# Hybrid decoder layer on one core: product 5 divided once more in group 18, with the reload of its quarter of x moved inside the group

## The chip, the cores and the metric

The kernel runs on one core of one Trainium2 chip. The metric is the device time of one execution in microseconds (us). Before the change the median of three runs is 1356.91 us, the lowest 1356.5 and the highest 1358.13.

## What is computed

One layer on x of 1024 tokens by 1024 features, all in float32:

```python
h = rmsnorm(x, norm_g[layer])
proj = h @ w_in[layer]                      # 1024 x 12288
b_a, c_a, x_a, z_a, q, k, v, z_b, g_a, g_b = split(proj)
y_a = short_conv_branch(b_a, c_a, x_a, z_a, conv_w, conv_b, w_a_out)
y_b = retention_branch(q, k, v, z_b, w_b_out)
x = x + (sigmoid(g_a) * y_a + sigmoid(g_b) * y_b) @ w_o
return rmsnorm(x, final_g)
```

The change touches only how a few columns of `h @ w_in` are computed.

## The kernel before, in words

**Products.** Every large matrix product is done by a Strassen-Winograd scheme: the matrix is cut in quadrants and seven products stand in for eight. Each float32 operand is split in a high and a low part, and a product is the sum of three matmuls (high by high, high by low, low by high; lines 2746, 2748 and 2749). The high part of the weights is made by ScalarE (`high`, line 1211), the low part by VectorE (`low`, lines 1755 and 1758), into three rotating slots: the parts of unit u can be made only when TensorE is done with unit u-3.

**Groups.** After the columns of v, the other columns of `w_in` are done in 20 groups (0 to 19) of 512 columns. Groups 0 and 1 hold a gate ("gate" groups), 2 to 9 the convolution ("conv"), 10 to 17 q, k and z_b ("turn": rotary turning and silu), 18 and 19 the other gate. In each group TensorE does the products in the order 1, 6, 2, 5, 7, 3, 4. A plain product is one unit of 24 matmuls of 512 columns.

**Divided products.** Some products are themselves cut in quarters and done by seven products of quarters: 42 matmuls of 256 columns, in two halves of 18 and 24, each with its own unit of weights (lines 2664 to 2666). Product 4 is divided in groups 1 to 18 (`TWICE`), product 3 in 2 to 9 (`THIRDS`), product 5 in 2 to 17 (`FIFTHS`). For a divided product POOL makes four sums of quarters of the weights (`second_sums`, lines 1027 to 1032) before the second half's parts can be made, and VectorE subtracts the shared quarters from the results (`second_first`, line 1913, once; `second_rest`, line 1926, three instructions) before it adds the product itself (`add`, lines 1905 and 1907).

**The x side.** Dividing product 5 needs four combinations of quarters of its x operand, T1 to T4. T3 takes the place of the operand's own quarter 1 in SBUF; the own quarter is kept in DRAM (`kept_d[2]`) and must be back before a plain product 5 runs. T1, T2 and T4 of products 4 and 5 share one area, `hx`: in each group of `FIFTHS` the ones of product 5 are loaded (`load_hx(5)`, lines 717 and 718, 0.5 and 1 MB) once product 4 of the group before has ended, and the ones of product 4 (`load_hx(4)`) once product 5 of this group has ended. TensorE waits for them by `t4_in` and `t1_t2_in`.

**Order of the work.** All orders are written out by hand. SyncE issues most transfers from one queue: in group g the parts of the next group's weights (line 628) as their buffers come free, and the stores of the results of group g-1 (`turn_stores`, lines 649, 700 and 701; `gate_stores`, line 649). ScalarE and VectorE each run one list in which unit u's place also carries work of the group before. Where `g in FIFTHS`, that list is another one: VectorE puts the turning of group g-1 in other places, and does `add(g, 3)` only behind `second_first` of product 4; ScalarE does the high parts of group g-1's second turn one unit later. ScalarE's evacuation of product 2 (`c11`, lines 1348 and 1349 in a turn group, line 1353 with a sigmoid in a gate group) stands at the unit of product 5; the high parts of the unit after next are made ahead of it, and those of the next unit again behind it. TensorE's product 7 waits for `c11_read`, product 3 for `add(g, 5)`, product 4 for `add(g, 7)`.

**After the groups.** From inside group 19 on the retention runs step by step. Its first transfers of q and k (`load_step`, line 784) wait until all stores of q, k and of group 18's gates have landed; its first scores (line 2782) are computed between products 5 and 7 of group 19.

Of the kernel before, what the change touches and what calls it, by code (L numbers as in the profile page):

```python
# [6 lines left out]
F32 = mybir.dt.float32  # L7
# [38 lines left out]
GROUPS = 20  # L46
# [2 lines left out]

TWICE = range(1, GROUPS - 1)  # L50
THIRDS = CONVS
FIFTHS = range(2, GROUPS - 2)
LAST_HALF, THIRD_HALF, FIFTH_HALF = 7, 8, 9
UNIT_TABLE = [(g, p) for g in range(GROUPS) for p in (0, 1, 2, 3, FIFTH_HALF, 4, 5, 6, LAST_HALF, THIRD_HALF)
              if (p != THIRD_HALF or g in THIRDS) and (p != LAST_HALF or g in TWICE) and (p != FIFTH_HALF or g in FIFTHS)]
UNITS = VALUE_UNITS + len(UNIT_TABLE)
# [49 lines left out]
def unit_at(g, product):  # L106
    return VALUE_UNITS + UNIT_TABLE.index((g, ORDER.index(product)))


def ended_at(g):  # L110

    return unit_at(g, 4) + (g in TWICE)


def third_ended_at(g):

    return VALUE_UNITS + UNIT_TABLE.index((g, THIRD_HALF if g in THIRDS else 5))


def fifth_ended_at(g):  # L120

    return unit_at(g, 5) + (g in FIFTHS)

# [6 lines left out]
def halved_product(g, product):  # L130

    return product == 4 and g in TWICE or product == 3 and g in THIRDS or product == 5 and g in FIFTHS

# [25 lines left out]
def summed_until(g):  # L159

    return 16 + g + (g > 0) + 4 * len([n for n in TWICE if n < g]) + 4 * len([n for n in THIRDS if n < g])\
        + 4 * len([n for n in FIFTHS if n < g])


def s2_made(g):

    return summed_until(g) + 1 + (g == 0)


def second_summed(g, product, n):  # L170

    return summed_until(g) + 1 + 4 * (product != 5 and g in FIFTHS) + 4 * (product == 3) + n


def second_added(g, product, n):

    before_g = 20 + 4 * (g - TWICE.start) + 4 * len([f for f in THIRDS if f < g])\
        + 4 * len([f for f in FIFTHS if f < g or f == g and product != 5])
    if g not in THIRDS or product == 5:
# [27 lines left out]
def kind_of(g):  # L207
    return "conv" if g in CONVS else "turn" if g in QZS else "gate"
# [123 lines left out]
def build(nc, x_t, columns, w_value, w_channel, w_last, x_rows, final_g, rope, tables, identity, out):  # L332
# [8 lines left out]
    kept_d = nc.dram_tensor("kept_scratch", (4, P, 2, 2, QUARTER), F32, kind="Internal").ap()  # L341
# [7 lines left out]
    def sem(name):  # L349
        return held.enter_context(nc.semaphore(name))  # L350
# [87 lines left out]
    w_hi, w_ready, unit_done = sem("w_hi"), sem("w_ready"), sem("unit_done")  # L438
# [45 lines left out]
    fifth_kept, t4_in, t1_t2_in = x_start, x_in[5], x_in[6]  # L484
# [26 lines left out]
    def made(name, count=2):  # L511

        return (8 if name == "raw" else 12) + 2 * MADE.index(name) + count

    def x_quarter(product, n, part):

        return hc[:, KEPT_AT[product], part, 2 * (n // 2):2 * (n // 2) + 2, n % 2 * QUARTER:(n % 2 + 1) * QUARTER]
# [40 lines left out]
    def _(sp):  # L558
# [67 lines left out]
        def load_work(g, role, quadrant):  # L626
            n = ROLES[g][role]
            sp.dma_start(work[n][:, :], w_channel[g, quadrant]).then_inc(work_in[n], 16)
# [86 lines left out]
        def load_hx(product):  # L715
            n = int(product == 5)
            sp.dma_start(hx[:, 2].bitcast(F32), hx_d[n, :, 2]).then_inc(t4_in, 16)
            sp.dma_start(hx[:, 0:2].bitcast(F32), hx_d[n, :, 0:2]).then_inc(t1_t2_in, 16)

        for g in range(GROUPS):  # L720
            if g == 1:
                sp.wait_ge(h_ready, made(3) + 4)
                for part, a in enumerate((t5_high, t5_low)):
                    sp.dma_start(hx_d[1, :, :, part], a[:, 0:3]).then_inc(fifth_kept, 16)
                    sp.dma_start(kept_d[3, :, part], a[:, 3]).then_inc(fifth_kept, 16)
                sp.wait_ge(fifth_kept, 112)
                sp.wait_ge(h_ready, made(3) + 4 + 3)
                sp.dma_start(hx_d[0], hx[:, :].bitcast(F32)).then_inc(fifth_kept, 16)
            if g == FIFTHS.start:
                sp.wait_ge(unit_done, unit_at(g - 1, 5) + 1)  # L730
                sp.wait_ge(fifth_kept, 128)
                for part in range(2):
                    sp.dma_start(x_quarter(5, 1, part).bitcast(F32), kept_d[3, :, part]).then_inc(fifth_kept, 16)
            if g in FIFTHS:
                sp.wait_ge(unit_done, ended_at(g - 1) + 1)
                load_hx(5)
            if g == FIFTHS.stop:
                sp.wait_ge(unit_done, fifth_ended_at(g - 1) + 1)
                for part in range(2):
                    sp.dma_start(x_quarter(5, 1, part).bitcast(F32), kept_d[2, :, part]).then_inc(fifth_kept, 16)  # L740
            if g == THIRDS.start:
                stores[kind_of(g - 1)](g - 1)
            if g + 1 < GROUPS:
                sp.wait_ge(w_ready, unit_at(g, 2) + 1)
                sp.wait_ge(summed, s2_made(g))
                load_work(g + 1, "a", 0)
            if g == TWICE.stop:
                sp.wait_ge(unit_done, ended_at(g - 1) + 1)
                for part in range(2):
                    sp.dma_start(x_quarter(4, 1, part).bitcast(F32), kept_d[0, :, part]).then_inc(kept_in, 16)  # L750
            if g == THIRDS.stop:
                sp.wait_ge(unit_done, third_ended_at(g - 1) + 1)
                for part in range(2):
                    sp.dma_start(x_quarter(3, 1, part).bitcast(F32), kept_d[1, :, part]).then_inc(third_kept, 16)
            if g + 1 < GROUPS:
                sp.wait_ge(w_ready, fifth_ended_at(g) + 1)
                load_work(g + 1, "e", 3)
                if g in FIFTHS and g in THIRDS:
                    sp.wait_ge(unit_done, fifth_ended_at(g) + 1)
                    load_hx(4)  # L760
                sp.wait_ge(w_ready, unit_at(g, 7) + 1)
                load_work(g + 1, "b", 2)
                if g in THIRDS and g > THIRDS.start:
                    stores[kind_of(g - 1)](g - 1)
                if g in FIFTHS and g not in THIRDS:
                    sp.wait_ge(unit_done, fifth_ended_at(g) + 1)
                    load_hx(4)
                if g in THIRDS:
                    sp.wait_ge(w_ready, ended_at(g) + 1)
                    load_work(g + 1, "d", 3)  # L770
                sp.wait_ge(w_ready, third_ended_at(g) + 1)
                load_work(g + 1, "c", 1)
            if g and g not in THIRDS:
                stores[kind_of(g - 1)](g - 1)
            if g + 1 < GROUPS and g not in THIRDS:
                sp.wait_ge(w_ready, ended_at(g) + 1)
                load_work(g + 1, "d", 3)
            if g == QZS.start:
                sp.wait_ge(y_out, 16 * len(CONVS))
                sp.dma_start(rope_sb[:, :, :], rope).then_inc(rope_in, 16)  # L780
# [2237 lines left out]
```

## Time and profile before

| | |
|---|---|
| median of 3 runs | 1356.91 us |
| profiled execution, its own time | 1357.59 us |
| its span | 1355.8 us |
| TensorE busy | 1344.9 us (99%) |
| VectorE, ScalarE, POOL busy | 1102.3, 622.7, 381.6 us |
| moved by DMA | 310.35 MB, mean 229 GB/s |

Times in rows are us from the start of the span, durations us as well unless ns is written. Matmul ends are modelled and overlap the next one, so the pace of TensorE is read from starts: from one matmul's start to the next one's. "ACT" is ScalarE, "DVE" VectorE, "SPq" SyncE's sequencer when it issues a DMA. In brackets stands how long the engine was idle before the instruction, and what released it.

### The profile page before, as it was taken

What the parts mean: (1) busy time and instruction counts of PE and PEld (TensorE: products, weight loads), DVE (VectorE), ACT (ScalarE), POOL (GpSimd) and SP (SyncE); (2) the same over time, 40 slices, a digit from 0 to 9 for tenths busy, and PEclk for the clock granted to TensorE, in tenths of its full rate; (3) what the DMA queues carried; (4) which work ended last, traced back from release to release, by engine and by line L of the source; (5) the groups of instructions that cost most, each with busy time, mean ns of one, the idle gap of its engine ahead of it and who ended that gap; (6) DMA issues with size and microseconds to landing.
All of it is one profiled execution on the core that took longest, in us unless ns stands there. A gap on an engine that the chain in (4) does not pass through costs nothing.

```text
span 1355.8 us, 18174 instructions
## 1 busy us (share of the span) xinstructions
PE 1344.9 (99%) x6930; PEld 1150.5 (85%) x6930; DVE 1102.3 (81%) x1179; ACT 622.7 (46%) x844; POOL 381.6 (28%) x411
## 2 busy tenths in 40 slices
PE   9999999999999999999999999999999999999997
PEld 8788888888898899888888888888888888888886
DVE  6898575688888888789999898748776998788887
ACT  7843243433333343333434443448778433434445
POOL 0100112344444554233343342225444001100002
PEclk9999999999999999999999999999999999999999
DMA  9746477867777777789999999866767689945443
GB/s 336 216 133 213 139 218 223 264 204 207 198 217 229 218 232 233 254 234 267 281 282 267 290 286 292 256 218 248 270 218 260 157 325 306 235 154 202 163 86 125
DMA packets 130534, 310.35 MB, mean 229 GB/s; under 512 B 9488, under 2 KB 54160, under 8 KB 121360
## 3 DMA queue, kind: packets, MB, share of 16 engines
q1 hardware_dynamic: 118928, 260.41, 55.0%
q0 software_dynamic: 11376, 48.76, 19.7%
q8 instruction: 55, 0.90, 0.3%
q14 instruction: 31, 0.25, 0.1%
q10 hardware_dynamic: 144, 0.02, 0.0%
HBM read 241.00 MB, written 59.77 MB: 222 GB/s over the span
## 4 chain that ended last, share of the span: by engine, by line
PE 88%; DVE 3%; ACT 2%; SPq 2%; issue 2%; DMA 2%; POOL 1%; POOLq 0%; DVEq 0%; ACTq 0%
PE psum L2748 12%; PE psum L2746 12%; PE psum L2749 12%; PE psum L2891 7%; PE psum L2889 7%; PE psum L2890 7%; PE psum L2664 5%; PE psum L2666 5%; PE psum L2665 5%; PE psum L2653 3%; PE psum L2655 3%; PE psum L2656 3%; PE psum L2791 2%; PE psum L2793 2%; PE psum L2792 2%
## 5 line engine op out<-in xcount | busy, mean ns | idle before, releaser
L1211 ACT ACTIVATE slots<-work 128x1024 fp32r<-128x1024 f32 (+1 forms) x182 | 182.4, 1011 | 407.4 <-POOL work L1032 145.8
L2748 PE MATMUL psum<-hc,slots 128*128 128x512 f32 x784 | 305.2, 389 | 0.0
L2746 PE MATMUL psum<-hc,slots 128*128 128x512 f32 x784 | 305.2, 389 | 0.0
L2749 PE MATMUL psum<-hc,slots 128*128 128x512 f32 x784 | 305.1, 389 | 0.0
L1504 ACT ACTIVATE last_slot<-arena 128x1024 fp32r<-128x1024 f32 x112 | 118.8, 1063 | 163.0 <-PE psum L2891 157.2
L2889 PE MATMUL psum<-last_slot 128*128 128x512 f32 (+1 forms) x452 | 175.3, 388 | 0.0
L2891 PE MATMUL psum<-last_slot 128*128 128x512 f32 (+1 forms) x452 | 175.0, 387 | 0.0
L2890 PE MATMUL psum<-last_slot 128*128 128x512 f32 (+1 forms) x452 | 175.0, 387 | 0.0
L2749 PEld LDWEIGHTS psum<-hc,slots 128*128 128x128 f32 x784 | 147.2, 188 | 30.8
L2746 PEld LDWEIGHTS psum<-hc,slots 128*128 128x128 f32 x784 | 147.2, 188 | 29.4
L2748 PEld LDWEIGHTS psum<-hc,slots 128*128 128x128 f32 x784 | 147.2, 188 | 29.3
L2094 DVE TENSOR_TENSOR last_slot<-arena,last_slot 128x1024 fp32r<-128x1024 f32 x112 | 135.8, 1223 | 31.1 <-ACT last_slot L1504 30.5
L1758 DVE TENSOR_TENSOR slots<-work,slots 128x1024 fp32r<-128x1024 f32 x116 | 136.6, 1183 | 13.4 <-ACT slots L1211 13.1
L2890 PEld LDWEIGHTS psum<-last_slot 128*128 128x128 f32 x452 | 84.9, 188 | 17.4
L2889 PEld LDWEIGHTS psum<-last_slot 128*128 128x128 f32 x452 | 84.9, 188 | 17.4
L2891 PEld LDWEIGHTS psum<-last_slot 128*128 128x128 f32 x452 | 84.9, 188 | 17.2
L2666 PE MATMUL psum<-hc,slots 128*128 128x256 f32 x336 | 94.9, 282 | 0.0
L2665 PE MATMUL psum<-hc,slots 128*128 128x256 f32 x336 | 94.7, 282 | 0.0
L2664 PE MATMUL psum<-hc,slots 128*128 128x256 f32 x336 | 94.6, 282 | 0.0
L2653 PE MATMUL psum<-slots,hc 128*128 128x512 f32 x224 | 88.3, 394 | 0.5 <-DVE slots L1758 0.5
L1755 DVE SCALAR_TENSOR_TENSOR slots<-work,slots 128x1024 fp32r<-128x1024 f32 (+1 forms) x66 | 75.6, 1146 | 16.1 <-ACT slots L1211 16.1
L1027 POOL TENSOR_TENSOR work<-work 128x256 f32<-128x256 f32 x42 | 39.8, 948 | 169.0 <-DVE slots L1755 109.8
(230 smaller groups left out, 2755.5 us busy)
## 6 DMA issues: line engine op xcount, KB each, us to landing
work<-w_channel SPq DMA_DIRECT2D x99, 512.0 KB, 5.4
hx<-hx_scratch SPq DMA_DIRECT2D x32, 1024.0 KB, 8.8
work<-w_channel POOLq DMA_DIRECT2D x59, 512.0 KB, 6.9
arena<-w_last SPq DMA_DIRECT2D x19, 1024.0 KB, 7.6
hx<-hx_scratch SPq DMA_DIRECT2D x32, 512.0 KB, 6.1
qk<-qk_scratch SPq DMA_DIRECT2D x32, 512.0 KB, 3.7
arena<-w_last POOLq DMA_DIRECT2D x9, 1024.0 KB, 11.3
v_raw<-value_scratch SPq DMA_DIRECT2D x32, 256.0 KB, 4.0
```

The source lines that it names most:

```text
L1211: nc.scalar.activation(slots[:, u % SLOTS, 0, 0:columns_of(u)], src, ACT.Copy, scale=-1.0 if negated(u) else 1.0).then_inc(w_hi, 1)
L1758: nc.vector.tensor_tensor(slot[:, 1, :], src, slot[:, 0, :].bitcast(F32), ALU.subtract).then_inc(w_ready, 1)
L2094: nc.vector.tensor_tensor(slot[:, 1, :, :], pair_at(group, product, j), slot[:, 0, :, :].bitcast(F32), ALU.subtract).then_inc(last_ready, 1)
L2664: nc.tensor.matmul(to, slot[:, 0, w], high, start=start and j == 0, stop=False, skip_group_check=True)
L2665: nc.tensor.matmul(to, slot[:, 0, w], low, start=False, stop=False, skip_group_check=True)
L2666: last = nc.tensor.matmul(to, slot[:, 1, w], high, start=False, stop=j == 1, skip_group_check=True)
L2746: nc.tensor.matmul(bank, slot[:, 0, w], x_high, start=product in STARTS and j == 0, stop=False, skip_group_check=True)
L2748: nc.tensor.matmul(bank, slot[:, 0, w], x_low, start=False, stop=False, skip_group_check=True)
L2749: last = nc.tensor.matmul(bank, slot[:, 1, w], x_high, start=False, stop=j == 3, skip_group_check=True)
L2889: nc.tensor.matmul(bank, l_high, r_high, start=start, stop=False, skip_group_check=True)
L2890: nc.tensor.matmul(bank, l_high, r_low, start=False, stop=False, skip_group_check=True)
L2891: return nc.tensor.matmul(bank, l_low, r_high, start=False, stop=stop, skip_group_check=True)
```

## The change

`FIFTHS` gains group 18, so that every place in the kernel that asks `g in FIFTHS` or `halved_product(g, 5)` now answers yes there. The load that brings product 5's own quarter back was issued first thing in group `FIFTHS.stop` (18); it is now issued in the last group of `FIFTHS` (again 18), behind `load_hx(4)`, and serves the plain product 5 of group 19.

```diff
@@ -49,7 +49,7 @@
 
 TWICE = range(1, GROUPS - 1)
 THIRDS = CONVS
-FIFTHS = range(2, GROUPS - 2)
+FIFTHS = range(2, GROUPS - 1)
 LAST_HALF, THIRD_HALF, FIFTH_HALF = 7, 8, 9
@@ -734,10 +734,6 @@
             if g in FIFTHS:
                 sp.wait_ge(unit_done, ended_at(g - 1) + 1)
                 load_hx(5)
-            if g == FIFTHS.stop:
-                sp.wait_ge(unit_done, fifth_ended_at(g - 1) + 1)
-                for part in range(2):
-                    sp.dma_start(x_quarter(5, 1, part).bitcast(F32), kept_d[2, :, part]).then_inc(fifth_kept, 16)
             if g == THIRDS.start:
                 stores[kind_of(g - 1)](g - 1)
@@ -765,6 +761,9 @@
                 if g in FIFTHS and g not in THIRDS:
                     sp.wait_ge(unit_done, fifth_ended_at(g) + 1)
                     load_hx(4)
+                if g == FIFTHS.stop - 1:
+                    for part in range(2):
+                        sp.dma_start(x_quarter(5, 1, part).bitcast(F32), kept_d[2, :, part]).then_inc(fifth_kept, 16)
                 if g in THIRDS:
                     sp.wait_ge(w_ready, ended_at(g) + 1)
                     load_work(g + 1, "d", 3)
```

## Rows read from the trace of the kernel before

**Rows 1.** The page: busy time by engine, and TensorE's granted clock in 40 slices.

```profile
PE 1344.9 (99%) x6930; PEld 1150.5 (85%) x6930; DVE 1102.3 (81%) x1179; ACT 622.7 (46%) x844; POOL 381.6 (28%) x411
...
PEclk9999999999999999999999999999999999999999
```

**Rows 2.** Windows of units, groups 17 and 18: length, busy by engine, clock, DMA, GB/s.

```profile
807.96:812.89 4.93, 4.93 (x44) 4.93 (x42) 4.49 (x7) 4.02 (x6) 0.15 (x1) 1.00 0.42 113
812.89:823.78 10.89, 10.89 (x50) 9.01 (x49) 10.58 (x13) 1.91 (x2) 5.76 (x6) 1.00 0.94 295
823.78:828.72 4.94, 4.94 (x44) 4.93 (x43) 4.27 (x6) 2.63 (x4) 0.29 (x1) 1.00 1.09 331
...
845.06:850.50 5.44, 5.44 (x26) 4.50 (x25) 4.61 (x7) 4.41 (x5) 0.00 (x0) 1.00 0.38 72
```

**Rows 3.** Timeline of ScalarE, group 17: start, length, instruction, idle before.

```profile
809.64 0.62 ACT L1388 ACTIVATE turn_b<-turn_a 128x512 fp32r<-128x512 f32 x1
...
811.12 1.05 ACT L1211 ACTIVATE slots<-work 128x1024 fp32r<-128x1024 f32 x1
...
824.88 0.62 ACT L1388 ACTIVATE turn_b<-turn_a 128x512 fp32r<-128x512 f32 x1
825.41 1.04 ACT L1211 ACTIVATE slots<-work 128x1024 fp32r<-128x1024 f32 x1
```

**Rows 4.** Timeline of ScalarE, group 18.

```profile
846.74 0.61 ACT L1388 ACTIVATE turn_b<-turn_a 128x512 fp32r<-128x512 f32 x1
847.37 1.28 ACT L1353 ACT_TABLE_LOAD   x1
848.67 1.03 ACT L1353 ACTIVATE tp_c<-psum 128x1024 f32<-128x1024 f32 x1
...
859.34 1.06 ACT L1361 ACTIVATE tp_v<-tp_v 128x1024 f32<-128x1024 f32 x1 [0.56 <-DVE tp_v L1907]
```

**Rows 5.** Timeline of VectorE, group 17 and the first unit of group 18.

```profile
812.21 1.23 DVE L1755 SCALAR_TENSOR_TENSOR slots<-work,slots 128x1024 fp32r<-128x1024 f32 x1 [0.36 <-ACT slots L1211]
813.35 2.46 DVE L1926 TENSOR_TENSOR tp_first<-tp_first,psum 128x768 f32<-128x768 f32 x3
815.92 1.23 DVE L1905 TENSOR_TENSOR tp_v<-psum,tp_first 128x1024 f32<-128x1024 f32 x1
...
820.82 1.21 DVE L1907 TENSOR_TENSOR tp_v<-tp_v,psum 128x1024 f32<-128x1024 f32 x1
...
824.23 1.22 DVE L1755 SCALAR_TENSOR_TENSOR slots<-work,slots 128x1024 fp32r<-128x1024 f32 x1
...
827.05 1.22 DVE L1758 TENSOR_TENSOR slots<-work,slots 128x1024 fp32r<-128x1024 f32 x1
...
832.33 1.23 DVE L1758 TENSOR_TENSOR slots<-work,slots 128x1024 fp32r<-128x1024 f32 x1
```

**Rows 6.** Timeline of POOL, groups 17 and 18.

```profile
818.10 1.10 POOL L1027 TENSOR_TENSOR work<-work 128x256 f32<-128x256 f32 x1 [4.47 <-DVE slots L1755]
...
821.58 0.74 POOL L1032 TENSOR_TENSOR work<-work 128x256 f32<-128x256 f32 x1
...
828.43 2.71 POOL L1014 TENSOR_TENSOR work<-work,work 128x1024 f32<-128x1024 f32 x1 [5.19 <-DVE slots L1758]
```

**Rows 7.** Timeline of SyncE's queue, groups 17 and 18; last, all 32 loads of line 718.

```profile
813.46 0.43 SPq L718 DMA_DIRECT2D hx<-hx_scratch  x1
...
833.59 1.07 SPq L740 DMA_DIRECT2D hc<-kept_scratch  x2
...
DMA to landing us min/median/max: 6.1/8.8/11.6
```

**Rows 8.** Timelines of SyncE's queue and of TensorE, group 19.

```profile
872.29 0.36 SPq L649 DMA_DIRECT2D gate_scratch<-tp_v  x1
879.32 0.33 SPq L784 DMA_DIRECT2D qk<-qk_scratch  x1
...
888.08 0.28 PE L2782 MATMUL psum<-qk 128*128 128x256 f32 x1
```

## The prediction

> **What bounds the kernel now.** I read the page first: TensorE is busy 99% of the span, at the full clock (the upper level, 2.4 GHz) in all 40 slices [rows 1]. So time goes only if TensorE gets less to do, and comes only if something makes it wait. The windows of the units come next [rows 2]. A divided unit takes 4.93 us (product 5 of group 17), a plain one 5.44 us (product 5 of group 18); two plain ones take 10.89, and busy equals length in every window: no bubble anywhere. Beside it the reader should see VectorE: in the two units behind product 5 of group 17 it is busy 10.58 of 10.89 us. That stretch decides what the change gives, so the timelines of ScalarE, VectorE and POOL come last [rows 3 to 6].
>
> Group 17 is turned into a ruler. Its product 5 starts at 807.96, that of group 18 at 845.05 to 845.06, so group 17's clock plus 37.10 is group 18's. I give the times of group 18 after the change on group 17's clock: group 18 will do what 17 does (both also finish a turn group), except where its own kind, gate, differs.
>
> **The saving.** One plain product (5.44) becomes one divided (4.93): -0.51 us of TensorE. The row of group 17 prices it, with the operands, queue and engines it will have in group 18.
>
> **What is added and hidden.** POOL makes four more sums, about 4.2 us by the same four behind product 4 (818.10 to 821.58 + 0.74) [rows 6], in the idle time that group 17 uses for them. ScalarE and VectorE make one more pair of parts; VectorE subtracts quarters four times more. All that is in group 17's timeline, which shows no wait of TensorE, so it costs nothing by itself. What hides it is VectorE's last slack.
>
> **The transfers.** SyncE issued the two reload DMAs at 833.59, 1.07 us together [rows 7]. In that place now stand the two of `load_hx(5)`, so the queue there is as long as before; landing at most 11.6 us after about 834.1 gives 845.7, and T1 is wanted at 845.06 + 2.11 = 847.2 (18 of the 42 matmuls, 18/42 x 4.93 = 2.11). `load_hx(4)` is issued at 813.46 + 37.10 = 850.56 for its 1 MB part, and wanted by the second half of product 4 at 845.06 + 4.93 + 10.89 + 2.11 = 862.99: 12.4 us, against 8.8 in the median and 11.6 at worst of 32 loads [rows 7]. The reload goes past the loads of parts a, e and b to stand behind it; it lands some 20 us before group 19's product 5. Queued behind its 1.07 us are part c of group 19, wanted some 20 us later, and the stores of group 17. Those slip by several us, and with them the wait before the first q and k load. That wait ended last on group 18's last gate store, issued at 872.29, the load following at 879.32, and the scores that need it come at 888.08 [rows 8]. The store will come about 2.5 us later (below); the load then goes out near 881.8 and takes some 4 to 7 us, before 889. Cost zero, 0 to 1 in the bounds.
>
> **Where group 18 differs from 17: the sigmoid.** ScalarE evacuates product 2 at the unit of product 5. In group 17 these are two short instructions between 809.64 + 0.62 and 811.12 [rows 3]. In group 18 a table load of 1.28 us comes first, then one of 1.03: from 847.37 to 849.70 [rows 4], or 812.60 on group 17's clock. Product 7 waits for it and is now due at 812.89: 0.3 us to spare, no cost. But ScalarE's next work, the high part for product 3, starts at 812.50 instead of 811.12: 1.38 later. Today that is free, since nobody on VectorE needs it early; in the divided order VectorE makes the low part of product 3 *ahead of* `second_rest` of product 5. In group 17 it was already waiting for ScalarE (0.36 us, low part at 812.21) and then ran without a gap to the low part of product 4's second half [rows 5]. So 1.39 us of delay travel down the whole run:
>
> 1. `second_rest` 813.35 becomes 814.74; `add(5)` 815.92 to 817.15 becomes 817.31 to 818.54. Product 3 wants it at 812.89 + 5.44 = 818.33. With some 0.05 for the handover TensorE waits **0.25 us**.
> 2. `add(7)` ends at 822.03 + 1.39 = 823.42; product 4 wants it at 823.78 + 0.25: no wait.
> 3. The low part of product 4's second half, 824.23 to 825.45, becomes 825.62 to 826.84. Wanted at 824.03 + 2.11 = 826.14: a wait of **0.75 us**.
> 4. The low part of product 1 of group 19 (827.05 to 828.27 in the ruler) needs ScalarE's high part, 825.41 in the ruler. It is later by 1.39, and by one gate instruction of 1.06 that a gate group puts ahead of it [rows 3, 4]: 827.80 to 828.85. Low part 828.88 to 830.10; wanted at 828.72 + 1.00 = 829.72. A wait of **0.42 us**.
> 5. The low part of product 6 needs POOL's S2, which runs 2.71 us behind step 4's low part [rows 6]: 830.25 to 832.96; high part to 834.0, low part to 835.4 (832.33 + 1.23 = 833.56 in the ruler [rows 5]). Wanted at 830.14 + 5.44 = 835.58: 0.2 us to spare. From there VectorE has no turning left and catches up.
>
> The sum: -0.51 + 0.25 + 0.75 + 0.42 = **+0.91 us**. The bounds of the waits: 0 if the 1.39 is absorbed (total -0.51), and for a longer chain the second-worst is every spare of 0.2 to 0.3 gone too (+0.7, total +1.6). I take the middle, since each term follows from rows of the same instructions. Against the profiled execution: 1357.59 + 0.91 = 1358.50. That execution lay 0.68 above the median, so as a median 1356.91 + 0.91 = **1357.8 us**. About 0.2% (2.7 us) is what a measurement of this kernel can tell from no change; the forecast lies within.
>
> **Rivals.**
>
> *A, the saving arrives whole.* If ScalarE's lateness does not reach TensorE, the time is 1356.91 - 0.51 = 1356.4. For it: group 17 has no wait at all, and a shift of VectorE against its neighbours may change how long its instructions take. Against it: VectorE had 0.31 us idle in those 10.89. Chance 0.22, with cases in between.
>
> *B, the table switch costs more than its row.* In the row the sigmoid starts 0.02 us behind the end of the table load (847.37 + 1.28, then 848.67) [rows 4]. If a further pause as long as the load came with it where the engine is pressed, all of steps 1 to 3 would start 1.28 us later: product 7 would wait 1.0 (812.60 + 1.28 against 812.89), product 3 then 0.5, the second half of product 4 0.7, and product 1 of group 19 0.4 as before. 1.0 + 0.5 + 0.7 + 0.4 - 0.5 = +2.1, so 1359.0. The Trainium skill, "ScalarE: Activation LUTs", section "What ACT_TABLE_LOAD costs", states such a pause: 1283 ns for the load plus about 1380 ns of drain, 2.66 us in all. The trace agrees on the load and shows no drain between it and the sigmoid. Chance 0.04.
>
> *C, slower: the exchange of combinations lands late.* The 1 MB of T1 and T2 for product 4 shares the engines with what is issued behind it: reload 0.5 MB, part c 0.5, four silu stores 1.0, q and k stores another 1.0 and more. At the 295 GB/s of that window [rows 2] 2 MB take 6.8 us, 3 MB 10.2. Served alongside, the load lands at 850.56 + 8.8 + 6.8 = 866.2 or at 869.6, TensorE waits 3.2 to 6.6 us, and the time is 1359.6 to 1363.0. It decides once the landing takes over 15.6 us; against it stands that 32 of 32 took at most 11.6 with the same company, bar the 0.5 MB. Chance 0.05.
>
> **How the numbers follow.** Forecast 0.62; A 0.22; B 0.04; C 0.05; small mixtures with an extra wait in group 19 but within 0.2% 0.05; a gain over 0.2% through some realignment that I don't see 0.02. Same: 0.62 + 0.22 + 0.04 + 0.05 = 0.93. Slower 0.05, faster 0.02. The range holds A with the scatter of the runs (0.4 below the median): 1356.4 - 0.5 = 1355.9, and B with as much scatter and a little of another wait: 1359.0 + 0.6 = 1359.6.
>
> **What the changed profile would show.** Product 5 of group 18 in 42 matmuls over 4.93 us; no table load but the one at about 847.4; `second_rest` of product 5 at 851.8 instead of 850.5; windows of group 18 with gaps of TensorE of about 0.25 ahead of product 3 (near 855.4), 0.75 inside product 4 (near 863.2) and 0.4 ahead of group 19's product 1 (near 866.8); group 19's product 1 starting 0.9 later than 866.30; all of it kept to the end. Line 718's new loads within 12 us. I am wrong if group 19 begins before 866.3, if a wait ends on a DMA, or if a gap opens in group 19 or at the first scores.

## The result, and the profile after

The changed kernel takes **1359.79 us** in the median of 12 runs (1358.55 to 1362.34); the kernel before, timed beside it, 1356.95. The ratio is 1.0023, with a 95% interval of 1.0015 to 1.003: about 0.2% slower, 2.8 us. The forecast was 1357.8 within 1355.9 to 1359.6, so the median lies 0.2 us above the range.

The windows of the changed kernel (columns as in [rows 2]): first group 18 and the part of group 19 up to the first scores, then product 5, products 7 and 3, and product 4 of group 18.

```profile
828.27:866.73 38.46, 37.84 (x206) 32.37 (x204) 33.52 (x39) 16.07 (x19) 13.64 (x12) 1.00 0.92 288
866.73:890.46 23.73, 22.06 (x96) 17.97 (x97) 13.86 (x14) 10.28 (x11) 3.60 (x2) 1.00 0.89 264
...
844.61:849.54 4.93, 4.93 (x43) 4.93 (x42) 2.97 (x5) 4.70 (x6) 0.89 (x1) 1.00 0.38 111
849.54:860.87 11.33, 11.18 (x50) 8.94 (x49) 10.40 (x11) 1.83 (x3) 4.68 (x5) 1.00 0.95 317
860.87:866.73 5.86, 5.38 (x43) 4.98 (x41) 4.75 (x8) 3.67 (x5) 0.30 (x1) 1.00 1.10 340
```

The same two stretches of the kernel before:

```profile
828.72:866.30 37.58, 37.58 (x188) 31.95 (x187) 30.47 (x35) 16.77 (x19) 11.29 (x9) 1.00 0.89 247
866.30:888.08 21.78, 21.78 (x99) 18.02 (x97) 10.54 (x10) 8.17 (x9) 1.07 (x2) 1.00 0.95 310
```

Product 5 is down to 4.93 us, as group 17's row said. But products 7 and 3 take 11.33 instead of 10.89 (+0.44), product 4 takes 5.86 instead of 4.93 (+0.93), and from the start of group 19 to the first scores 23.73 us pass instead of 21.78 (+1.95). The sum is -0.51 + 0.44 + 0.93 + 1.95 = +2.8 us, as much as the medians differ. These are the rows of one execution, of 1360.26 us. (The spans, 1358.3 against 1355.8, differ by 2.5: this execution came to group 18 0.45 us earlier and lost 0.1 us behind the first scores.) Group 18 alone costs 0.9 us net; group 19, which the diff hardly touches, costs twice that.

TensorE in the timeline shows where the waits end:

```profile
855.30 0.47 PE L2745 MATMUL psum<-hc,slots 128*128 128x512 f32 x1
...
863.53 0.38 PE L2663 MATMUL psum<-hx,slots 128*128 128x256 f32 x1 [0.36 <-DVE slots L1754]
...
866.73 0.50 PE L2745 MATMUL psum<-hc,slots 128*128 128x512 f32 x1
...
890.46 0.36 PE L2781 MATMUL psum<-qk 128*128 128x256 f32 x1 [1.67 <-DMA qk<-qk_scratch]
```

Lines stand one lower than before. Product 3 started 0.14 us behind the end of `add(5)` (853.93 + 1.23 in the rows below), the second half of product 4 waited for VectorE's low part, group 19's product 1 for the next low part, and the first scores for the transfer of q and k.

Each wait costs a little more than its gap. Behind it the first two matmuls start 0.31 to 0.34 us apart where 0.23 is usual (512 columns), or 0.22 where 0.12 is usual (256 columns). Read from starts, the gaps themselves are 0.30, 0.52, 0.27 and 1.83 us; about 0.1 us behind each makes up the rest.

ScalarE and VectorE in group 18 (timelines; they answer to [rows 3 to 5]):

```profile
846.93 1.28 ACT L1352 ACT_TABLE_LOAD   x1
848.22 1.03 ACT L1352 ACTIVATE tp_c<-psum 128x1024 f32<-128x1024 f32 x1
849.14 1.78 ACT L1210 ACTIVATE slots<-work 128x1024 fp32r<-128x1024 f32 x2
...
863.43 1.04 ACT L1360 ACTIVATE tp_v<-tp_v 128x1024 f32<-128x1024 f32 x1
864.38 1.04 ACT L1210 ACTIVATE slots<-work 128x1024 fp32r<-128x1024 f32 x1
```

```profile
850.23 1.22 DVE L1754 SCALAR_TENSOR_TENSOR slots<-work,slots 128x1024 fp32r<-128x1024 f32 x1 [1.73 <-ACT slots L1210]
851.37 2.46 DVE L1925 TENSOR_TENSOR tp_first<-tp_first,psum 128x768 f32<-128x768 f32 x3
853.93 1.23 DVE L1904 TENSOR_TENSOR tp_v<-psum,tp_first 128x1024 f32<-128x1024 f32 x1
...
862.26 1.22 DVE L1754 SCALAR_TENSOR_TENSOR slots<-work,slots 128x1024 fp32r<-128x1024 f32 x1
...
865.45 1.23 DVE L1757 TENSOR_TENSOR slots<-work,slots 128x1024 fp32r<-128x1024 f32 x1 [1.04 <-ACT slots L1210]
```

On group 17's clock the low part of product 3 starts at 850.23 - 37.10 = 813.13 in an execution that is 0.45 early, so 813.58: the forecast had 813.60. The sequence that VectorE then runs is the forecast's, to 0.1 us.

SyncE's queue, from the exchange (`load_hx(4)`) to the first step's load:

```profile
850.10 0.89 SPq L718 DMA_DIRECT2D hx<-hx_scratch  x1
...
867.31 0.85 SPq L649 DMA_DIRECT2D qk_scratch<-tp_v  x1
...
869.68 0.69 SPq L701 DMA_DIRECT2D qk_scratch<-turn_a  x1
870.42 1.14 SPq L628 DMA_DIRECT2D work<-w_channel  x1
871.60 0.97 SPq L746 DMA_DIRECT2D hc<-kept_scratch  x2
...
874.40 1.27 SPq L649 DMA_DIRECT2D gate_scratch<-tp_v  x1
887.00 0.33 SPq L783 DMA_DIRECT2D qk<-qk_scratch  x1
```

Group 18's last gate store goes out at 874.40, 2.1 us later than in [rows 8]; with the 0.45 that is the 2.5 of the forecast. But the load behind it goes out at 887.00, not 881.8: the store took 12.6 us to land instead of 7.0. In the kernel before, the second set of group 17's turn stores began at 858.21:

```profile
858.21 0.36 SPq L649 DMA_DIRECT2D qk_scratch<-tp_v  x1
```

Here it begins at 867.31, right ahead of part d, the reload of product 4's quarter and the gate stores. The windows of the transfers (last two columns: busy share of the 16 DMA engines, GB/s) show where the work went. The changed kernel:

```profile
855.00:860.00 5.00, 4.85 (x22) 3.90 (x22) 5.00 (x7) 0.00 (x0) 3.81 (x4) 1.00 1.03 406
...
875.00:880.00 5.00, 5.00 (x23) 4.13 (x22) 3.28 (x3) 2.11 (x3) 0.00 (x0) 1.00 0.99 265
```

The kernel before:

```profile
855.00:860.00 5.00, 5.00 (x23) 4.13 (x22) 4.30 (x5) 2.88 (x4) 4.29 (x5) 1.00 0.60 147
...
875.00:880.00 5.00, 5.00 (x24) 4.14 (x23) 2.36 (x2) 1.06 (x1) 0.00 (x0) 1.00 0.74 196
```

Before, the engines had idle time at 855 to 860 and again at 875 to 880, where SyncE sat waiting for a store that was nearly alone. After the change both stretches are full.

### The profile page after: what moved, and what is told of

The parts are those of the page before. It is cut to its first block, busy times and chain, and to the rows that moved or that the text cites. A ratio compares the mean times of both kernels' runs of the same rounds, so it can differ in the third digit from the quotient of the medians.

```text
span 1358.3 us, 18229 instructions
## 1 busy us (share of the span) xinstructions
PE 1345.3 (99%) x6948; PEld 1151.4 (85%) x6948; DVE 1107.6 (82%) x1184; ACT 621.7 (46%) x845; POOL 385.8 (28%) x415
## 4 chain that ended last, share of the span: by engine, by line
PE 91%; DVE 3%; DMA 2%; issue 2%; ACT 2%; POOL 1%; POOLq 0%; SPq 0%; DVEq 0%; ACTq 0%
PE psum L2747 12%; PE psum L2745 12%; PE psum L2748 12%; PE psum L2889 7%; PE psum L2890 7%; PE psum L2888 7%; PE psum L2663 5%; PE psum L2665 5%; PE psum L2664 5%; PE psum L2652 4%; PE psum L2655 4%; PE psum L2654 4%; PE psum L2790 2%; PE psum L2792 2%; PE psum L2791 2%
## 5 line engine op out<-in xcount | busy, mean ns | idle before, releaser
L2745 PE MATMUL psum<-hc,slots 128*128 128x512 f32 x776 | 302.3, 390 | 0.3
L2747 PE MATMUL psum<-hc,slots 128*128 128x512 f32 x776 | 302.1, 389 | 0.0
L2748 PE MATMUL psum<-hc,slots 128*128 128x512 f32 x776 | 302.0, 389 | 0.0
L2748 PEld LDWEIGHTS psum<-hc,slots 128*128 128x128 f32 x776 | 145.7, 188 | 30.5
L2745 PEld LDWEIGHTS psum<-hc,slots 128*128 128x128 f32 x776 | 145.7, 188 | 29.9 <-issue 0.5
L2747 PEld LDWEIGHTS psum<-hc,slots 128*128 128x128 f32 x776 | 145.7, 188 | 28.9
L2665 PE MATMUL psum<-hc,slots 128*128 128x256 f32 x344 | 97.2, 282 | 0.0
L2664 PE MATMUL psum<-hc,slots 128*128 128x256 f32 x344 | 96.9, 282 | 0.0
L2663 PE MATMUL psum<-hc,slots 128*128 128x256 f32 x344 | 96.9, 282 | 0.0
L2652 PE MATMUL psum<-slots,hc 128*128 128x512 f32 x224 | 88.2, 394 | 0.0
L2655 PE MATMUL psum<-slots,hc 128*128 128x512 f32 x224 | 87.2, 389 | 0.0
```

The lines of the kernel that those rows point to most:

```text
L2652: nc.tensor.matmul(bank, x_high, w_high, start=product in starts and i == 0 and kk == 0, stop=False, skip_group_check=True)
L2655: last = nc.tensor.matmul(bank, x_low, w_high, start=False, stop=i == 1 and kk == 1, skip_group_check=True)
L2663: nc.tensor.matmul(to, slot[:, 0, w], high, start=start and j == 0, stop=False, skip_group_check=True)
L2664: nc.tensor.matmul(to, slot[:, 0, w], low, start=False, stop=False, skip_group_check=True)
L2665: last = nc.tensor.matmul(to, slot[:, 1, w], high, start=False, stop=j == 1, skip_group_check=True)
L2745: nc.tensor.matmul(bank, slot[:, 0, w], x_high, start=product in STARTS and j == 0, stop=False, skip_group_check=True)
```

## The experiments

Each was timed in five rounds beside the kernel before on the same chip; that kernel's median there stands beside it. "Wait at the scores" is the length from group 19's first matmul to the first scores, less the 21.78 us of the kernel before.

Two questions were put apart, the waits in group 18 and the wait at the scores. **D**: the table load ahead of the sigmoid makes VectorE late, which gives the three waits in group 18. It is the forecast's own. For the wait at the scores three theories stood: W (3 MB more bytes), Q (SyncE's wait for the gate stores), O (group 17's turn is finished later in the divided order, so its stores fall on the others).

### e1_table_early: no table load on the critical stretch

```diff
                         silu(g - 1, 3)
+                        if g == QZS.stop:
+                            nc.scalar.activation(small[:, 41:42], eps[:, 0:1], ACT.Sigmoid)
```

> The changed kernel, but ScalarE does a sigmoid of one column behind the second silu of group 17's results (early in group 18), so that the table load of 1.28 us falls in an idle stretch there and no longer ahead of the sigmoid of product 2. Theory D (the divided order puts VectorE's low part of product 3, and with it second_rest and all behind it, behind the table load): the waits of TensorE ahead of product 3 (0.44 us) and inside product 4 (0.55) vanish, the one ahead of group 19's product 1 (0.38) shrinks to 0 to 0.1, so group 18 takes 37.1 us instead of 38.46; the wait at the first scores of group 19 (1.7 to 1.9) stays or grows, since the gate stores have less time: 1 us or so is gained, about 1358.8 as a median. Rival (the waits come from the transfers or from POOL's four more sums): group 18 stays at 38.4 us and the time at 1359.8.

Measured: 1361.44 us (6 runs) against 1357.18, ratio 1.0031 (1.0019 to 1.0043). Its windows and its table load:

```profile
828.66:865.76 37.10, 37.10 (x207) 32.40 (x205) 33.66 (x39) 16.27 (x20) 13.63 (x12) 1.00 0.93 285
865.76:890.11 24.35, 21.98 (x98) 17.91 (x97) 14.49 (x14) 10.27 (x11) 3.60 (x2) 1.00 0.93 280
```

```profile
836.61 1.28 ACT L1644 ACT_TABLE_LOAD   x1
```

Group 18 takes 37.10 us without a gap: all three waits are gone at once, by moving 1.28 us of ScalarE. D is shown. And nothing came of it: the first scores start at 890.11 instead of 890.46, with 2.57 us of wait instead of 1.95, because the q and k load comes when it comes. The 1 us of gain that I expected was missed. The median is even higher than the changed kernel's, though the two intervals overlap. The profiled execution, at 1359.8 us, is the fastest of the six. The other five took 1361.2 to 1361.6 us, and their mean granted clock is 0.997 where its own is 0.998. A stretch at TensorE's lower clock behind the longer wait, as it is seen in e14_small_deferred below, could do that, but no trace shows it here.

### e2_qk_early: the first load no longer waits for the gate stores

```diff
-        sp.wait_ge(tp_out[0], 16 * tp_stored(GROUPS - 2))
+        sp.wait_ge(tp_out[0], 16 * tp_stored(GROUPS - 4))
...
             load_step(s)
+        sp.wait_ge(tp_out[0], 16 * tp_stored(GROUPS - 2))
         stores[kind_of(GROUPS - 1)](GROUPS - 1)
```

> The changed kernel, but the first four loads of q, k and v wait for the stores of group 16 and 17 only (and for all stores of q and k), not for group 18's gate stores; the wait for those stands behind the four loads. Theory Q (the 1.95 us lost in group 19 are the first load of q and k, held back by the landing of group 18's last gate store): the load goes out near 880 instead of 887.0, lands before 888.8, TensorE has no wait at the first scores, and the time is 1.9 us less, about 1357.8 (the forecast's number). Rival (the load would be late anyway, since the queues are full of group 17's stores): load issued before 883 but landed after 889, gain under 0.5 us.

Measured: 1358.18 against 1357.18, ratio 1.0009 (1.0 to 1.0018). The load went out at 878.22 and took 9.4 us (3.9 in the kernel before); the wait at the scores is 21.90 - 21.78 = 0.1 us. Q holds: some 1.8 of the 2.8 us are back. What is left of the median is about group 18's net cost. (In this profile group 18 took 39.5 us, with a wait ahead of product 7 that e11_turn_early explains below.)

### e3_both and e4_before_both

> Both edits together on the changed kernel. Theories D and Q together: no wait in group 18 (37.1 us) nor at the first scores; the saving of 0.51 us arrives whole, 1356.4 us as a median, ratio to the kernel before 0.9996. Rival: some third cause, then at least 0.5 us of wait stays in groups 18 or 19.

> Control: both edits on the kernel before, product 5 of group 18 plain. Both theories: nothing, since that kernel has neither wait: group 18 takes 37.6 us, 1356.9 us, ratio 1.000. If it is faster by 1 us or more, the edits bring something of their own and e3_both says nothing of the change.

Measured: e3_both 1357.77, ratio 1.0002 (0.9994 to 1.0011); e4_before_both 1357.16 against the same 1357.18, ratio 1.0001 (0.9993 to 1.001). So the edits bring nothing by themselves, and on the changed kernel they take back nearly all. The window of e3_both from group 19 to the scores:

```profile
866.47:889.15 22.68, 21.99 (x98) 17.90 (x97) 12.81 (x13) 9.87 (x11) 3.60 (x2) 1.00 1.01 309
```

Group 18 is at 37.10, but 0.9 us go at the scores: the load went out at 877.90 and landed 11.1 us later, in queues that are busy all the time (share 1.01). The 0.51 us did not arrive; 1356.4 was missed.

### e5_no_exchange and e6_no_reload: fewer bytes

Both leave out transfers, so one product runs on the wrong combination or quarter of x and the layer's result is not computed; only their times are used.

```diff
                     sp.wait_ge(unit_done, fifth_ended_at(g) + 1)
-                    load_hx(4)
+                    if g != FIFTHS.stop - 1:
+                        load_hx(4)
```

(with `hx_loads(18, 4)` one lower), and for e6_no_reload:

```diff
-                if g == FIFTHS.stop - 1:
-                    for part in range(2):
-                        sp.dma_start(x_quarter(5, 1, part).bitcast(F32), kept_d[2, :, part]).then_inc(fifth_kept, 16)
...
-                pe.wait_ge(fifth_kept, 192)
+                pe.wait_ge(fifth_kept, 160)
```

> The changed kernel with load_hx(4) of group 18 left out (1.5 MB): product 4 of group 18 is computed with product 5's T1, T2 and T4, all its work and its waits stay. Theory W (the q and k load is late because 3 MB more go through queues that are full from 850 us on, so that everything behind them lands later): the last gate store lands several us earlier, the first q and k load goes out before 884 instead of 887, the wait at the first scores falls from 1.7 to 0.3 at most, the time by 1.3 to 1.9 us to 1358.0 to 1358.5. Rival O (the stores of group 17 are late because the divided order turns its second half later on VectorE and ScalarE, whatever the bytes): the load goes out at 886 or later, the wait stays over 1 us, the time over 1359.2. Group 18 itself keeps its 38.4 us by both.

> The changed kernel with the reload of product 5's own quarter left out (0.5 MB, two transfers of SyncE): the plain product 5 of group 19 runs on T3 in its place. Theory W: a third of the effect of leaving out the 1.5 MB, a gain of 0.3 to 0.7 us. Rival (the place of the reload, behind the exchange and ahead of group 17's stores, is what costs): the gain is 1.5 us or more. Theory O: no gain.

Measured: 1359.61 and 1359.9 against 1357.45, ratios 1.0012 (1.0003 to 1.002) and 1.0013 (1.0002 to 1.0024). Queue and window of e5_no_exchange:

```profile
875.66 1.21 SPq L649 DMA_DIRECT2D gate_scratch<-tp_v  x1
887.62 0.33 SPq L784 DMA_DIRECT2D qk<-qk_scratch  x1
```

```profile
868.18:891.07 22.89, 22.05 (x96) 17.97 (x97) 13.02 (x13) 10.03 (x11) 3.61 (x2) 1.00 0.82 244
```

With 1.5 MB less the last gate store still takes 12 us to land, the load still goes out at 887.6, and 1.1 us of wait remain (0.9 in e6_no_reload, with its load at 888.27). Group 18 keeps its 38.5 us in both. The medians are 2.2 and 2.5 us above the kernel before. W is not the main cause; whether the bytes have a part of 0.3 to 1 us can't be told, since the ratios' intervals overlap the changed kernel's, and 0.5 MB left out does as much as 1.5.

### e9_before_late_turn: one part of the change alone

On the kernel before, ScalarE's and VectorE's splitting of group 17's second turn is put where the divided order has it, and nothing else:

```diff
-                    if p == (5 if g in FIFTHS else 4):
+                    if p == (5 if g in FIFTHS or g == QZS.stop else 4):
                         turned(g - 1, 1)
...
                     second_first(g, product_at(n))
+                    if n == 6 and g == QZS.stop:
+                        turned(g - 1, 1)
...
-                    if p == 4 and g not in FIFTHS:
-                        turned(last, 1)
```

> The kernel before, product 5 of group 18 plain, with one part of the change alone: in group 18 the second half of group 17's turn is split in parts as late as the divided order does it (ScalarE one unit later, VectorE behind second_first of product 4), so that its four stores of q and k (1 MB in packets of 512 bytes) go out at 866 to 869 instead of 858 to 861, right ahead of part d, the reload and group 18's gate stores. Theory O: the last gate store, issued at 872 to 874, lands 10 us or more later; the first q and k load goes out at 883 or later instead of 879.3; TensorE waits 0.3 to 1.5 us at the first scores, the time rises by as much, to 1357.3 to 1358.5. Rival W (bytes): nothing changes, load at 879 to 880, no wait.

Measured: 1360.42 against 1357.83, ratio 1.0019 (1.0002 to 1.0035): 2.6 us slower. The profiled execution is the slowest of the twelve (1367.98 us; the others took 1358.46 to 1366.53). It lost 6.5 us at about 697 to 706, long before group 18 and the edit: a wait of 3.0 us for VectorE, then TensorE at half its clock (0.50) until about 706. So its times in group 18 stand 6.5 us later. Windows, queue, and the row of TensorE's waits:

```profile
835.26:872.85 37.59, 37.59 (x189) 31.96 (x188) 30.41 (x34) 16.52 (x19) 10.97 (x9) 1.00 0.86 230
872.85:896.83 23.98, 21.94 (x99) 17.87 (x97) 13.78 (x14) 9.22 (x10) 1.06 (x2) 1.00 0.78 232
```

```profile
874.20 0.36 SPq L649 DMA_DIRECT2D qk_scratch<-tp_v  x1
...
880.82 0.73 SPq L649 DMA_DIRECT2D gate_scratch<-tp_v  x1
893.17 0.33 SPq L784 DMA_DIRECT2D qk<-qk_scratch  x1
```

```profile
PE psum L2782 <- DMA qk<-qk_scratch: 2.0, 1, 2.0
```

Group 18 is untouched (37.59), no product is divided, no byte is added, and yet the last gate store lands 12.4 us after its issue and TensorE loses 2.2 us at the scores. That is the missing term, made on the kernel before by the lateness of four stores of 256 KB. O is shown as a cause that is enough by itself; the part of the bytes stays open, as said.

### e16_late_turn_qk_early: by which way

> e9_before_late_turn (kernel before, group 17's second turn late) with the relaxed wait ahead of the first q and k load. If the loss goes through that wait: the load goes out near 878, the wait at the first scores falls from 2.0 us to 0 to 0.5, the time is back at the kernel before's, ratio 1.000 to 1.0005. Rival (the full queues alone make the load late): 1 us or more of wait stays, ratio 1.001 or more.

Measured: 1357.3 against 1357.64, ratio 1.0 (0.9991 to 1.0008). Group 19 to the scores, and the load:

```profile
866.09:887.86 21.77, 21.77 (x98) 18.02 (x97) 11.78 (x12) 8.16 (x9) 1.06 (x2) 1.00 0.92 285
```

```profile
877.17 0.33 SPq L784 DMA_DIRECT2D qk<-qk_scratch  x1
```

With the relaxed wait TensorE has no wait between 828 and 900, and the late turn costs nothing. So the chain is: turn finished late, stores late, gate stores in one bunch with them, SyncE held by the landing of the last one, q and k load late.

### e11_turn_early and e12_after_again

```diff
-                            turned(g - 1, 1, range(1))
+                            turned(g - 1, 1, range(1 + (g == QZS.stop)))
                         low(u + 1)
-                        if g - 1 in QZS:
+                        if g - 1 in QZS and g != QZS.stop:
...
-                if p == 5:
+                if p == (6 if g == QZS.stop else 5):
                     gate(g, tp_v2, 7)
```

> The changed kernel with two swaps in group 18: ScalarE makes the high part of group 19's product 1 ahead of the sigmoid of product 7's result, and VectorE does both low parts of group 17's second turn ahead of product 1's low part. Theory D: the third wait of TensorE (0.38 us ahead of group 19) vanishes, the first two (0.44, 0.55) stay. Theory O: the last four turn stores go out 2 us earlier, and the wait at the first scores falls from 1.95 to 0.5 to 1.5 us. Together 0.8 to 1.8 us less than the changed kernel. Rival: the wait at the scores does not move, 0.4 us less at most.

> The changed kernel itself once more, beside the others on the same chip, to anchor them: 1359.8 us, waits of 0.44, 0.55 and 0.38 us in group 18 by all theories, since they hang on orders and durations; the wait at the first scores between 0.6 and 2.5, since it hangs on a landing behind full queues.

Measured: e11_turn_early 1361.5 against 1357.83, ratio 1.0028 (1.0018 to 1.0038); e12_after_again 1360.43, ratio 1.0022 (1.0008 to 1.0036), the first result again. Its two stretches took 39.00 and 23.52 us, together 3.2 us more than in the kernel before; in the first profile it was 2.8.

Both profiles, and that of e2_qk_early, also show a wait ahead of product 7 for the sigmoid (0.84, 0.23 and 0.74 us), which the first one did not: the 0.3 us to spare of the forecast are too few in some executions. The traces show why. VectorE can start to turn the first half of group 17's results only when a store of the turn before it (`turn_a`, line 701) has landed. In e11_turn_early:

```profile
838.05 0.69 DVE L2019 TENSOR_TENSOR turn_a<-tp_first,rope_sb 128x512 f32<-128x512 f32 x1 [2.73 <-DMA qk_scratch<-turn_a]
...
850.92 0.47 PE L2745 MATMUL psum<-hc,slots 128*128 128x512 f32 x1 [0.84 <-ACT tp_c L1352]
```

VectorE's idle time before this instruction was 2.73 us here, 2.20 in e2_qk_early and 1.66 in e12_after_again; it started at 835.52 without idle time in the first profile. ScalarE then waited 0.4 to 1.0 us for the turned results ahead of its high parts, and the table load and the sigmoid stand behind those.

In e11_turn_early the wait ahead of group 19 is gone, as D expected (matmuls start 0.11 us apart there). The rest of the expected gain was missed: the wait at the scores stayed at 1.95 us (1.74 in e12_after_again). The first of the last four turn stores went out at 867.73 (868.86 in e12_after_again), not 2 us earlier: SyncE was still issuing the store ahead of it, which took 3.97 us. The load went out at 888.16 as against 888.14.

### e7, e8, e10 and e13 to e15: can the transfers be moved apart?

All on top of e3_both, but e8, which is on e4_before_both. e7_deferred and e8_before_deferred issue part d, the reload of product 4's quarter and the gate stores behind step 0's load; e10_steps_first behind step 1's; e14_small_deferred moves only part d and the reload, behind all four steps; e13_three adds e11's swaps; e15_all is e13 and e14. The edit of e7_deferred, cut to its core (the same lines are taken out where they stood):

```diff
+        stores[kind_of(GROUPS - 2)](GROUPS - 2)
+        load_step(1)
+        sp.wait_ge(w_ready, ended_at(GROUPS - 2) + 1)
+        load_work(GROUPS - 1, "d", 3)
+        for part in range(2):
+            sp.dma_start(x_quarter(4, 1, part).bitcast(F32), kept_d[0, :, part]).then_inc(kept_in, 16)
+        for s in range(2, AHEAD):
             load_step(s)
```

> e3_both, and in group 19 the reload of product 4's quarter (0.5 MB), part d of group 19 (0.5 MB) and group 18's four gate stores (2 MB) are issued behind the first load of q, k and v instead of ahead of it. Theory W: that load, which took 11.2 us to land in e3_both behind these 3 MB, lands in 4 to 7 us, by 885; no wait at the first scores, no wait in group 18; 1356.4 to 1356.7 us, 0.3 to 0.6 us under the kernel before. Rival: the later stores then hold up another transfer (steps 2 and 3, the silu loads), and 0.5 us or more are lost again between 890 and 940.

> Control: the same edits (table load early, relaxed wait, deferred transfers) on the kernel before. It has no wait at the first scores, so theory W expects nothing: 1356.9 us, ratio 1.000. e7_deferred should be 0.5 us under this one, the plain saving of the divided product.

> e7_deferred with the loads of steps 0 and 1 and the table both ahead of the deferred transfers (in e7_deferred step 1's load stood behind the gate stores, and VectorE came late for keys at 896). If the lateness of step 1 was what e7_deferred lost again: no wait of TensorE over 0.2 us between 845 and 915, 1356.5 to 1357.0 us, at or below the kernel before. Rival: steps 2 and 3 or the silu loads are late next, waits of 0.5 us or more near 905 to 925, and 1358 or more.

> e3_both (table load early, relaxed wait) with e11_turn_early's two swaps. With the table load gone VectorE has its 1.4 us back, so the swaps cost nothing and the last four turn stores go out some 2 us earlier: the first q and k load lands 1 to 2 us earlier than the 11.2 us of e3_both, no wait at the first scores, 1356.4 to 1357.0 us, ratio 0.9995 to 1.000. Rival: the load's landing hangs on all that is queued, not on those four stores, and a wait of 0.5 us or more stays (ratio 1.0002 or more).

> e3_both with part d of group 19 and the reload of product 4's quarter (1 MB together) issued behind the first four steps' loads instead of ahead of group 18's gate stores; the gate stores stay in their place. First load lands 2 to 3 us earlier than in e3_both, no wait at the first scores; both moved transfers are wanted only near 900: 1356.4 to 1357.0 us. Rival: part d lands too late for product 4 of group 19 (near 903), a new wait there of 0.5 us or more.

> The edits of e13_three and e14_small_deferred together. Theories D and O: no wait in groups 18 and 19, the 0.51 us arrive, 1356.4 us, ratio 0.9996. Rival: another transfer is late next, 1357.5 or more.

| | median | before beside it | ratio (95%) |
|---|---|---|---|
| e7_deferred | 1358.82 | 1357.45 | 1.0005 (0.9991 to 1.0019) |
| e8_before_deferred | 1359.23 | 1357.45 | 1.0011 (1.0001 to 1.002) |
| e10_steps_first | 1362.56 | 1357.83 | 1.004 (1.0025 to 1.0055) |
| e13_three | 1358.11 | 1357.64 | 1.0002 (0.9993 to 1.0011) |
| e14_small_deferred | 1361.32 | 1357.64 | 1.0027 (1.0016 to 1.0038) |
| e15_all | 1361.97 | 1357.64 | 1.0032 (1.002 to 1.0044) |

The deferrals did what they were for: in e7, e10, e14 and e15 the first scores come with no wait (21.77 to 21.83 us). But in each a new wait came, for keys, near 896 us (901 in e10, whose profile is 5 us late). It was 0.69 us in e7, 1.61 in e10, 2.04 in e14, 3.40 in e15, and 2.26 in e8 on the kernel before, where none had been. In e14_small_deferred:

```profile
883.49 0.43 SPq L628 DMA_DIRECT2D work<-w_channel  x1
...
893.15 1.06 ACT L1211 ACTIVATE slots<-work 128x1024 fp32r<-128x1024 f32 x1 [8.54 <-DMA work<-w_channel]
...
896.74 0.80 PE L2793 MATMUL psum<-v_parts,keys 128*128 128x512 f32 x1 [2.04 <-DVE keys L2059]
```

The same ScalarE instruction in the kernel before:

```profile
888.28 1.06 ACT L1211 ACTIVATE slots<-work 128x1024 fp32r<-128x1024 f32 x1 [3.27 <-PE psum L2749]
```

So it is not the next step's load that was late, but the deferred part d itself. It landed 9.6 us after its issue, and ScalarE, which runs its list in order, wanted it for a high part at 888.3 and not "near 900"; its work on the keys stands behind that high part. The profiles of e7, e8, e10 and e15 show the same row, with ScalarE idle for 7.18 to 9.89 us until part d landed. (e14's rival had part d late, but for product 4 near 903.) All five deferred part d; no run left it in its place and deferred only the gate stores, so that way stays untested.

The waits do not account for all that these versions lost. In e14, with TensorE still for 2.2 us before, the next eight matmuls start 0.43 us apart and not 0.23 (the first pair 0.60). TensorE ran there at half its clock, the lower level of 1.2 GHz (last columns: granted clock, then DMA share and GB/s), which cost another 1.7 us:

```profile
896.74:899.90 3.16, 3.16 (x8) 2.48 (x8) 1.48 (x3) 1.85 (x4) 0.20 (x1) 0.50 0.00 0
```

The profile of e15 shows the same from 897.31 on, and that of e9_before_late_turn from 897.60 on, 0.8 us behind its wait at the scores. The profiles of e1 and e8 have waits of 2.5 and 2.4 us without it. The profiled execution of e10_steps_first also lost 5 us near 695 to 705, ahead of every edit, and its twelve executions spread over 10.6 us; why its median is 4.7 us up is open.

e13_three, which defers nothing, still has 0.7 us at the scores. No version here beats the kernel before; e3_both, e7_deferred and e13_three can't be told from it.

## Why the prediction was wrong

- **The saving** (-0.51): right, 5.44 to 4.93.
- **Added work hidden, exchange in time**: right. The two loads by line 718 around product 5 landed without a wait (9.0 us for the one at 850.10). Rival C did not happen.
- **Steps 1 to 4, the table load behind which VectorE is late**: right in kind and size. Forecast 0.25 + 0.75 + 0.42 = 1.42 us, measured 0.44 + 0.93 = 1.37 us, and e1_table_early removes all of it. VectorE's instructions come within 0.1 us of the forecast. That the sums agree so well is in part luck: the gaps alone are 0.30 + 0.52 + 0.27 = 1.09 us, and the rest is the slower pace of TensorE's first matmuls behind each wait, which the forecast did not have.
- **The sigmoid, "0.3 us to spare, no cost"**: right in the first profile, not in three others, where product 7 waited 0.23 to 0.84 us. The forecast took VectorE's turning from one execution and did not ask what lets it start, the landing of a store.
- **Rival B**: no. The load again ends at 848.21 and the sigmoid starts at 848.22. The Trainium skill ("ScalarE: Activation LUTs", "What ACT_TABLE_LOAD costs") gives 1283 ns for the load and about 1380 ns of drain. The traces agree on the load, a mean of 1283 ns, and show no drain: in all six profiles of the changed order in which this load stands ahead of the sigmoid, the sigmoid starts 0.01 to 0.02 us behind the load's end.
- **The step that failed** is the transfers' "Cost zero, 0 to 1 in the bounds". I had the store's issue right (2.5 us later), and took from [rows 8] that the rest stays: 7.0 us from the issue to the next load, then 4 to 7 us. But those 7.0 us belonged to a store that was nearly alone. Its three fellows had gone out 4 us earlier, and group 17's last turn stores 12 to 14 us earlier. In the changed order all of these, part d and the reload go out between 867 and 876, and the q and k load follows the last store after 12.6 us. I had written that "those slip by several us", and did not ask what they slip onto. The ruler had the answer: in group 17, whose order is the divided one, the last four stores of the turn before begin at 828.90, which is 866.00 on group 18's clock and 7.8 us behind the 858.21 of the plain order. I used the ruler for the engines and not for SyncE's stores.

```profile
828.90 1.33 SPq L649 DMA_DIRECT2D qk_scratch<-tp_v  x1
```

The term is +1.95 us (e9_before_late_turn makes 2.2 alone) and decides the result: without it the forecast of group 18 gives 1357.8, and the relaxed wait of e2_qk_early measures 1358.18.
- **Rival A** (all of it hidden) was further off than the forecast. No rival held the mechanism that came; rival C had transfers delay each other, but put the wait at product 4's combinations. The forecast's own signs of being wrong did name it, "if a wait ends on a DMA, or if a gap opens in group 19 or at the first scores", and the profile has both. A chance of 0.05 stood on an extra wait in group 19, without a mechanism.

## What to carry to other kernels

When a change moves a store later, ask what it now lands beside, and take its time to land from a row in which the queues are as full as they will be, not from one where they had drained. Look for a wait that asks for more than it needs: here the first load waited for stores whose data it does not read, harmless until they slipped. Where two delays lie one behind the other, as VectorE's here and the q and k load's, removing the first may pay nothing, because the second sets the next start (e1_table_early). And before a transfer is deferred, find the first instruction that wants it in the list of each engine that works in order, not only the product that uses it last.

## What was not expected of the hardware

A 512 KB store landed in 6.9 us with the three like it issued about 4 us ahead (kernel before). It took 11.8 to 12.5 us (changed kernel, e12, e5, e9) when SyncE issued 4 MB within 9 us, this store the last of them, with or without another 1.5 MB some 20 us earlier.

After a wait TensorE's first two matmuls start about 0.1 us further apart than usual. Behind waits of 2.2 to 3.6 us near 895 its granted clock fell to 0.50 for about 3 us in three profiles (e9, e14, e15). It stayed at 1.00 behind 2.5 and 2.4 us in two others (e1, e8), so the length of the wait alone does not decide it.

The changed kernel's 12 runs span 3.8 us, those of the kernel before beside them 1.8. That a transfer which sets the pace makes the runs scatter is not shown by this: beside the experiments the kernel before spans 5.1 to 7.4 us in 24 to 35 runs.
